# Sample pages of a paged attention: value pages issued by GpSimd, key pages by SyncE, and the next head's maps moved behind key pages

## The reference, cut to what matters

```python
def diff_attend(q, k, v, q_pos, k_pos, lam):
    s = jnp.einsum('bqhcd,bkhcd->bhcqk', q, k) / math.sqrt(DIFF_HEAD_DIM)
    s = jnp.where(k_pos[None, :] <= q_pos[:, None], s, -jnp.inf)
    p = jax.nn.softmax(s, axis=-1)
    attn = p[:, :, 0] - lam * p[:, :, 1]
    return jnp.einsum('bhqk,bkhe->bqhe', attn, v)

def diff_sample(q, k, v, lam, k_pool, v_pool, page_table):
    k_past = k_pool[page_table].reshape(B, -1, DIFF_HEADS, 2, DIFF_HEAD_DIM)
    v_past = v_pool[page_table].reshape(B, -1, DIFF_HEADS, DIFF_V_DIM)
    k_all = jnp.concatenate([k_past, k], axis=1)
    v_all = jnp.concatenate([v_past, v], axis=1)
    return diff_attend(q, k_all, v_all, past + jnp.arange(T), jnp.arange(past + T), lam)
```

## Time and profile before

| | us |
|---|---|
| median of 3 runs | 4800.99 (4799.27 to 4809.54) |
| time of the profiled execution | 4808.47 |
| its span | 4806.5 |
| attention phase, layer 0, first page issue to last value group | 1443.8 to 2114.2 |
| attention phase, layer 1, the like | 3832.0 to 4497.0 |

### The profile page before, as it was taken

One profiled execution on the slowest core, in us unless ns is written; L12 is line 12 of the kernel. 1 busy time (PEld: TensorE's weight loads), 2 busy tenths in 40 slices (PEclk: granted clock), 3 DMA queues, 4 the chain that ended last, 5 costly groups with the idle time before them and its releaser, 6 DMA issues.

```text
span 4806.5 us, 113485 instructions
## 1 busy us (share of the span) xinstructions
PE 4082.4 (85%) x49138; PEld 3556.3 (74%) x49138; DVE 2046.6 (43%) x4539; ACT 1739.4 (36%) x3551; POOL 514.4 (11%) x273
## 2 busy tenths in 40 slices
PE   7999997888878888877989999968888688888678
PEld 7999996777765555556979999967777555555578
DVE  6111112666645555552231111136666455455445
ACT  2000002666655565541110000026666555655311
POOL 5232230000000000011032223200000000000201
PEclk9999997899988999987999999979999899999789
DMA  3121111111114354343222112111111243444342
GB/s 134 67 76 71 67 72 58 35 44 41 32 49 150 97 165 130 92 141 124 86 81 76 67 67 76 62 65 38 37 41 32 71 150 91 158 128 123 101 138 86
DMA packets 222341, 410.46 MB, mean 85 GB/s; under 512 B 32146, under 2 KB 132500, under 8 KB 207764
## 3 DMA queue, kind: packets, MB, share of 16 engines
q1 hardware_dynamic: 206868, 313.75, 20.7%
q10 hardware_dynamic: 14976, 89.46, 4.7%
HBM read 296.39 MB, written 106.76 MB: 84 GB/s over the span
## 4 chain that ended last, share of the span: by engine, by line
PE 68%; DVE 12%; ACT 8%; issue 5%; SPq 3%; DMA 3%; POOL 0%; DVEq 0%; ACTq 0%
PE psum L2040 10%; PE psum L2042 10%; PE psum L2043 10%; PE psum L1364 4%; PE psum L1392 3%; PE psum L714 3%; PE psum L1595 3%; PE psum L1596 3%; PE psum L1597 3%; PE psum L1380 2%; PE psum L1128 2%; PE psum L711 2%; ACT arena L1168 2%; SPq L989 1%; PE psum L785 1%
## 5 line engine op out<-in xcount | busy, mean ns | idle before, releaser
L2040 PE MATMUL psum<-x_hi,w_parts 128*128 128x416 f32 x2640 | 933.1, 353 | 45.7 <-POOL w_parts L1961 21.1
L2043 PE MATMUL psum<-x_hi,w_parts 128*128 128x416 f32 x2640 | 926.9, 351 | 0.0
L2042 PE MATMUL psum<-x_lo,w_parts 128*128 128x416 f32 x2624 | 921.3, 351 | 0.0
L1973 DVE TENSOR_TENSOR arena<-psum,arena 128x416 f32<-128x416 f32 x330 | 195.1, 593 | 1239.0 <-PE psum L2043 1234.9
L333 ACT ACTIVATE arena<-arena 128x256 f32<-128x256 f32 x16 | 8.2, 513 | 1477.3 <-DVE arena L457 1477.3
L2040 PEld LDWEIGHTS psum<-x_hi,w_parts 128*128 128x128 f32 x2640 | 497.0, 188 | 53.9 <-POOL w_parts L1961 23.2
L1271 DVE TENSOR_SCALAR_CACHE_REDUCE arena<-psum 128x512 f32<-128x512 f32 (+3 forms) x640 | 357.7, 608 | 351.1 <-PE psum L1364 220.8
L2043 PEld LDWEIGHTS psum<-x_hi,w_parts 128*128 128x128 f32 x2640 | 497.4, 188 | 6.5
L2042 PEld LDWEIGHTS psum<-x_lo,w_parts 128*128 128x128 f32 x2624 | 494.7, 189 | 4.9 <-issue 0.6
L1392 PE MATMUL psum<-arena 128*128 128x128 f32 x2176 | 311.9, 285 | 64.0 <-ACT arena L1177 46.7
L1364 PE MATMUL psum<-arena 64*128 64x512 f32 (+3 forms) x1280 | 324.3, 610 | 39.9 <-DVE arena L1271 21.8
(11 more groups left out here) (352 smaller groups left out, 6835.0 us busy)
## 6 DMA issues: line engine op xcount, KB each, us to landing
out_proj_t<-arena ACTq DMA_DIRECT2D x66, 1040.5 KB, 4.1
arena<-in_cache_k SPq DMA_DIRECT2D x256, 256.0 KB, 2.8
arena<-in_cache_v SPq DMA_DIRECT2D x256, 256.0 KB, 3.0
arena<-in_w_in SPq DMA_DIRECT2D x66, 512.0 KB, 3.5
arena<-out_proj_t SPq DMA_DIRECT2D x96, 257.0 KB, 3.3
arena<-out_proj_t SPq DMA_DIRECT2D x24, 1024.0 KB, 6.9
x_res<-in_x SPq DMA_DIRECT2D x10, 1664.0 KB, 17.2
m_raw<-mixed_t SPq DMA_DIRECT2D x10, 1664.0 KB, 7.6
```

The lines of the kernel that those rows point to most:

```text
L1973: dve.tensor_tensor(ost[:, b % 2, 1 + g * TG:1 + (g + 1) * TG], bank[q % banks_of(l)][:, 0:TG], RSTD[:, cols(g)], ALU.mult).then_inc(p_ev, 1)
L2040: pe.matmul(bank[q % n][:, 0:TG], w_hi[:, b % 3, k, :], x_hi[:, k, cols(g)], start=(k == 0), stop=False)
L2042: pe.matmul(bank[q % n][:, 0:TG], w_hi[:, b % 3, k, :], xl, start=False, stop=False)
L2043: mm = pe.matmul(bank[q % n][:, 0:TG], w_lo[:, b % 3, k, :], x_hi[:, k, cols(g)], start=False, stop=(k == KT - 1))
```

## The change

Reading the numbers of value pages and issuing their transfers goes from SP to POOL: `values_sync` becomes `value_page`, and a new function `attn_gpsimd` calls it for all 16 pages of all 8 sequences in order, with the same wait for `pv_done` before each group. SP is left with key pages and maps. Key pages 4 to 15 are now issued one after the other; for odd b below 7 the next head's query map comes behind the key page with index 12 (the 13th) and its key map behind the one with index 14 (the 15th), and the next head's values behind the last key page, as before. The two semaphores `u_v` are no longer cleared between phases, so PE's wait for them counts on over both layers.

```diff
-        u_k, u_v = [csem(f"page_k{i}") for i in range(KS)], [csem(f"page_v{i}") for i in range(2)]
+        u_k, u_v = [csem(f"page_k{i}") for i in range(KS)], [sem(f"page_v{i}") for i in range(2)]
...
-        def values_sync(sp, l, b, gs):
-            for g in gs:
-                n = b * 4 + g
-                if n >= 2:
-                    sp.wait_ge(pv_done, n - 1)
-                for p in range(4 * g, 4 * g + 4):
-                    pg = sp.value_load(ptab[0:1, b * NP + p:b * NP + p + 1], min_val=0, max_val=N_PHYS - 1)
-                    sp.dma_start(vpg[:, n % 2 * 4 + p % 4, :], ins["cache_v"][bass.ds(l * N_PHYS + pg, 1)].rearrange("n p c -> (n p) c")).then_inc(u_v[n % 2], 16)
+        def value_page(pool, l, b, q):
+            n = b * 4 + q // 4
+            if n >= 2 and q % 4 == 0:
+                pool.wait_ge(pv_done, n - 1)
+            pg = pool.value_load(ptab[0:1, b * NP + q:b * NP + q + 1], min_val=0, max_val=N_PHYS - 1)
+            pool.dma_start(vpg[:, n % 2 * 4 + q % 4, :], ins["cache_v"][bass.ds(l * N_PHYS + pg, 1)].rearrange("n p c -> (n p) c")).then_inc(u_v[n % 2], 16)
...
-        def load_maps(sp, l, h):
-            if h:
+        def load_map(sp, l, h, i):
+            if h and i == 0:
                 sp.wait_ge(s_ok, first(NT * (h - 1)) + 1)
-            for i, r in enumerate((Q_ROW, K_ROW)):
-                sp.dma_start(kq[h % 2][:, i, :], map_rows(l, h, r)).then_inc(c_kq, 16)
+            sp.dma_start(kq[h % 2][:, i, :], map_rows(l, h, (Q_ROW, K_ROW)[i])).then_inc(c_kq, 16)
...
-            load_maps(sp, l, 0)
+            for i in range(2):
+                load_map(sp, l, 0, i)
...
             keys_sync(sp, l, 0, range(KS))
             for b in range(NSEQ):
                 h = b // 2
-                keys_sync(sp, l, b, range(KS, 8))
-                values_sync(sp, l, b, (0, 1))
-                if b % 2 and h + 1 < HEADS:
-                    load_maps(sp, l, h + 1)
-                keys_sync(sp, l, b, range(8, NP))
-                if b % 2 and h + 1 < HEADS:
+                ahead = b % 2 and h + 1 < HEADS
+                for p in range(KS, NP):
+                    keys_sync(sp, l, b, (p,))
+                    if ahead and p in (12, 14):
+                        load_map(sp, l, h + 1, (p - 12) // 2)
+                if ahead:
                     load_values(h + 1)
                 if b + 1 < NSEQ:
                     keys_sync(sp, l, b + 1, range(KS))
-                values_sync(sp, l, b, (2, 3))
+
+        def attn_gpsimd(pool, l):
+            pool.wait_ge(u_in, U_IN)
+            for b in range(NSEQ):
+                for q in range(NP):
+                    value_page(pool, l, b, q)
...
-                pe.wait_ge(u_v[n % 2], 64 * (n // 2 + 1))
+                pe.wait_ge(u_v[n % 2], 64 * (n // 2 + 1 + l * NSEQ * 2))
...
                 rwkv_gpsimd(pool, l)
                 ph.end(pool, l, 1)
+                attn_gpsimd(pool, l)
                 ph.end(pool, l, 2)
```

More of the change, by code:

```diff
@@ L1098, in beside_vector, with beside_tensor @@
                 dve.tensor_tensor(u_st[:, 6:7], u_st[:, 9:10], u_st[:, 8:9], ALU.mult).then_inc(coef_ok, 1)
-        def beside_tensor(pe, b, k):
+        def beside_tensor(pe, l, b, k):
             if b == 0 and k == 4:
@@ L1411, in beside @@
                 for b, k in pieces(t, j):
-                    beside_tensor(pe, b, k)
+                    beside_tensor(pe, l, b, k)
             for t in range(NTILE + 2):
```

## The result

The changed kernel took 4774.85 us in the median of six runs (4769.36 to 4788.45). Against the runs of the kernel before (4809.8 us in the median of six) the ratio is 0.9936, with a 95% interval of 0.9917 to 0.9954: some 31 us faster, between 22 and 40. (The ratio goes by the means, 4776.9 and 4807.9 us; the two medians lie 35.0 us apart.) The sign was forecast, and the time lies in the range; the gain is two thirds of the 45.3 us forecast, or three quarters by the medians. The profiled execution took 4769.4 us, 39.1 less than the profiled one before; 30.9 of that lie in the two attention phases, and the rest in phases that the change doesn't touch, whose length varies from run to run by as much.

What follows compares the result with a forecast made beforehand. PE was taken to set the pace, losing 64.8 us to waits for key and value pages. 49.1 + 9.0 - 12.8 = 45.3 us off gave 4756 us against the median of 4801.0; 8-in-10 range 4735 to 4850.

Steps and rivals of the forecast that it cites:

- The maps' term: Key pages 4 to 15 of six odd sequences: maps moved behind key pages 12 and 14 take off 49.1 us.
- the eight value pages': Key pages 8 and 9, no longer behind eight value pages on SP, save 9.0 us over eight odd sequences.
- Rival C: Key pages 13 to 15 late behind maps (4774), or ACT and DVE take back half the 58 us (4785); chance 0.12.
- Rival B: DVE and POOL hinder each other in attention, 0.18 us more a value page: 23 us, time 4779; chance 0.10.
- POOL's term: Value groups 2 and 3 of 16 sequences: POOL's pace of 1.20 us a page against SP's 1.10 costs 12.8 us.
- rival A: POOL's pace well above 1.6 us, lengthening waits before group 3; midway 106 us dearer, time 4849; chance 0.28.
- my eight steps of 0.1: Value groups 2 and 3: eight page issues by POOL, each 0.1 us slower than SP's, over 16 sequences: 12.8 us.

Runs made afterwards that it cites:

- two reads: The changed kernel with every page number read twice by POOL; measured 4850.2 us in one run, attention phases 1378.6 us.

## Why the prediction was right, and where it was off

**The maps' term (49.1 us) and the eight value pages' (9.0) were right together.** The odd stretches fell by 59.9 us where I had 58.1. The way to that number, comparing equal work with and without maps in the same trace, counts the clock in; the waits alone (49.7 us for key pages before) would have given less. The run with the maps moved alone gives the terms one by one: 47.9 us off in the odd stretches, and 12 more with POOL. But the first term isn't the maps' alone. POOL with the maps left in place takes off 48 us there too, since key page 8 was late by the maps and by the eight value pages issued ahead of them, together.

**No key page was pushed behind a map**, as worked out: in layer 0 a moved map went from issue to landing in 5.3 us in the median (6.5 at most; 7.1 to 9.6 before), and the waits for key pages are 0.9 us in all. Rival C's first half is out. So is its second: DVE and ACT took nothing back in the odd stretches, which are shorter than sequence 7's had been. Rival B is out as well: POOL's 256 issues take 0.536 us at the minimum and in the median, and all but two take 0.545 or less (0.707 at the most), though a DVE instruction ran beside 136 of them; and DVE's busy time did not change. The exception that the Trainium skill (SBUF — State Buffer, Who interferes with whom) makes for DVE's instruction with an accumulator agrees: it ran beside 82 issues, and none of these took over 0.545 us.

**The step that failed is POOL's term: 12.8 us forecast, 35.0 measured** (31.6 against the run with the maps moved alone, whose own 14 stretches are 3.4 us longer than those before). The sum came near because the odd stretches gave what was forecast, and because some 6 us fell off elsewhere, by luck. The term has three parts.
- The issuing came out near, and in part by luck. The pace was 1.15 us, where I took 1.20, so rival A is out. But POOL also starts later: 0.42 us more from group 0's end to its first issue, which I hadn't priced by itself. Both together are 0.61 us a sequence, where my eight steps of 0.1 gave 0.8: 9.8 us in place of 12.8.
- The landing, for which I took what SP's pages have, was not the same: 0.84 us later for the last page in the mean (1.1 by the medians), 13.4 us in 16 sequences. With the issuing that makes 1.45 us a sequence, 23 us, and the waits grew by 21.0. The sentence on the first byte of the Trainium skill (DMA: Bandwidth & Descriptors, Latency and other measured facts) had pointed the right way; its 0.4 us would have given 6 of the missing microseconds. The trace has 0.3 us for the first page of group 2. The rest builds up over the eight pages, and most of it is in the last one, which flies together with SP's next key pages. The runs with the groups split between POOL and SP show the same: pages of both engines land later when they fly together. How much is owed to that, and how much to POOL's pages following one another, stays open: no run had POOL issue eight pages with SP silent.
- I put nothing for the clock between sequences. It is below 1.00 in 3 of the 14 stretches before and in 8 after, and PE's busy time there grew by 15.4 us. A stretch of the longer kind takes 38.1 us at 1.00 and 41.1 at 0.92, so a fall costs 3 us, and five more falls about 15. From the windows of the kernel with SP and three buffers:

```profile
1969.50:2007.60 38.10, 33.21 (x347) 1.00 0.36 114
...
3990.30:4031.40 41.10, 36.40 (x348) 0.92 0.34 108
```

With waits of up to 5.8 us (two reads) all 14 stretches are below 1.00. But without any value wait there are still 4 (POOL, three buffers) and 6 (SP, three buffers). What part of the 15 us is owed to the longer waits, and what to how the work falls in time, stays open; no run held the one fixed and moved the other.

**The starting point was right:** there was no reserve in the supply of groups 2 and 3. I had then priced the steps of the supply and left out its head and its tail.

## What to carry to other kernels

When eight transfers must be read, issued and landed between two points on the path, price the whole way to the last landing, and treat the start and the landing on another engine's queue as no better known than its pace. Look also at what the relieved queue will now send at the same time. Before moving issues to another engine, try the order on the queue that has them: here moving the maps back by a few key pages gave 51 us of the phases, and moving 256 issues to another engine as well took 20 of them back, net. And where a supply has no reserve, one more buffer (here 8 KB a partition) did more than any division of the issuing: with it, it no longer mattered who issued.

## What the runs showed of the hardware that I had not expected

A page issued by POOL landed 3.8 us after its issue in the median, against 3.0 for SP's, though POOL's instruction (0.54 us) is only 0.2 us longer than SP's (0.34). Within a run of eight pages at 1.15 us the landing grew from 2.94 to 4.13 us; at 1.7 us it grew to 3.43; SP's, at 1.10 us, stayed between 2.96 and 3.13 after the first. Two queues at once delay both: key pages of SP that were issued among POOL's landed after 4.07 us instead of 2.68. POOL's pages went in fewer packets: 67.13 MB in 20480 packets, as the page after has it, 80 a page and about 3.3 KB each, for rows of 2 KB. SP's queue lost 36864 packets with the same pages (206868 to 170004), 144 a page.

```profile
q0 software_dynamic: 20480, 67.13, 4.3%
```
